# Gate sums in the prompt attention: column groups of 512 filled in two halves, one weight buffer split between groups

## The reference

```python
h = jnp.einsum('bsd,de->bse', x, w_in)     # D_MODEL 1024; the last 3*1024 columns are the gates
...
up = jnp.einsum('bsnw,nwd->bsnd', br, w_br)
mixed = (jax.nn.sigmoid(gates.reshape(B, S, 3, D_MODEL)) * up).sum(axis=2)
y = jnp.einsum('bsd,de->bse', mixed, w_o)
return _layernorm(ALPHA * x + y, ln_g, ln_b)
```

## Time and profile before

| | us |
|---|---|
| median of three runs (lowest, highest) | 3657.45 (3652.4, 3669.2) |
| the profiled execution's own time | 3665.47 |
| its span in the profile | 3663.8 |
| mean granted TensorE clock in it | 0.957 |
| TensorE matmuls busy | 3297.0, 90% of the span |
| TensorE weight loads busy | 2687.0, 73% |
| VectorE, ScalarE, GpSimd busy | 1449.7, 897.0, 172.7 |

### The profile page before, as it was taken

The page is one execution under the profiler, slowest core; times in us unless marked ns, Lnnn a source line. Parts: engine busy times, 40 slices in busy tenths (PEclk is TensorE's granted clock), DMA queues, the critical chain, the costliest instruction groups (busy, mean ns, idle before and its releaser), DMA issues. The chain is left out here.

```text
span 3663.8 us, 52922 instructions
## 1 busy us (share of the span) xinstructions
PE 3297.0 (90%) x20910; PEld 2687.0 (73%) x20910; DVE 1449.7 (40%) x3559; ACT 897.0 (24%) x2006; POOL 172.7 (5%) x118
## 2 busy tenths in 40 slices
PE   0999987999999997889969999789999999887988
PEld 0788876777777775677758888767777787755877
DVE  5214234444444442254631143444444434324446
ACT  1221212333223332120212212223332233322010
POOL 0000000101110100000000000010111110000000
PEclk9999998999999998899979999889999999988999
DMA  5322226322332317653342222352223332196433
GB/s 196 109 88 94 85 63 200 76 67 61 87 93 81 90 34 202 206 222 132 136 155 90 91 95 68 114 159 66 77 68 85 94 85 63 35 266 224 182 135 109
DMA packets 405678, 419.78 MB, mean 115 GB/s; under 512 B 155072, under 2 KB 314688, under 8 KB 403072
## 3 DMA queue, kind: packets, MB, share of 16 engines
q1 hardware_dynamic: 371600, 376.88, 33.2%
q10 hardware_dynamic: 33840, 39.66, 3.3%
HBM read 291.17 MB, written 127.64 MB: 114 GB/s over the span
## 5 line engine op out<-in xcount | busy, mean ns | idle before, releaser
L1069 PE MATMUL att_gacc<-att_gwh,keep_xh 128*128 128x256 f32 x1728 | 507.6, 294 | 6.8 <-POOL att_gwl L989 6.8
L351 PE MATMUL proj_acc<-proj_wh,keep_xh 128*128 128x512 f32 (+1 forms) x1296 | 502.1, 387 | 12.4 <-DVE proj_wl L326 12.4
L353 PE MATMUL proj_acc<-proj_wh,keep_xl 128*128 128x512 f32 (+1 forms) x1296 | 501.0, 387 | 0.0
L352 PE MATMUL proj_acc<-proj_wl,keep_xh 128*128 128x512 f32 (+1 forms) x1296 | 500.9, 387 | 0.0
L1071 PE MATMUL att_gacc<-att_gwh,keep_xl 128*128 128x256 f32 x1728 | 489.0, 283 | 0.0
L1070 PE MATMUL att_gacc<-att_gwl,keep_xh 128*128 128x256 f32 x1728 | 488.4, 283 | 0.0
L1095 ACT ACTIVATE att_p<-att_ss,att_stat 128x257 f32<-128x257 f32 (+9 forms) x384 | 249.4, 650 | 681.6 <-DVE att_stat L1145 681.6
L1023 PE MATMUL att_ss<-att_kt,att_qt 64*128 64x256 f32 (+9 forms) x1024 | 376.2, 469 | 1.4 <-DVE att_kt L1080 1.4
L1069 PEld LDWEIGHTS att_gacc<-att_gwh,keep_xh 128*128 128x128 f32 x1728 | 329.2, 191 | 22.9 <-issue 10.6
L1070 PEld LDWEIGHTS att_gacc<-att_gwl,keep_xh 128*128 128x128 f32 x1728 | 329.0, 190 | 0.0
L1071 PEld LDWEIGHTS att_gacc<-att_gwh,keep_xl 128*128 128x128 f32 x1728 | 328.1, 190 | 0.0
(11 more groups left out here) (291 smaller groups left out, 4450.3 us busy)
## 6 DMA issues: line engine op xcount, KB each, us to landing
scratch_gates<-att_gout SPq DMA_DIRECT2D x216, 128.0 KB, 1.7
up_gates<-scratch_gates SPq DMA_DIRECT2D x18, 1536.0 KB, 7.9
proj_raw<-in_w_in SPq DMA_DIRECT2D x48, 512.0 KB, 3.7
att_graw<-in_w_in SPq DMA_DIRECT2D x48, 512.0 KB
str_ka<-in_cache_a_kT SPq DMA_DIRECT2D x16, 1024.0 KB, 9.6
str_va<-in_cache_a_v SPq DMA_DIRECT2D x16, 1024.0 KB, 5.4
scratch_sg<-proj_out SPq DMA_DIRECT2D x54, 256.0 KB, 2.0
up_br<-scratch_br SPq DMA_DIRECT2D x54, 256.0 KB, 8.1
```

Source lines behind the costliest of these rows:

```text
L351: nc.tensor.matmul(bank, hi, wh[:, u, kt, 0:w], start=kt == 0, stop=False)
L352: nc.tensor.matmul(bank, hi, wl[:, u, kt, 0:w], start=False, stop=False)
L353: mm = nc.tensor.matmul(bank, lo, wh[:, u, kt, 0:w], start=False, stop=kt == KT - 1)
L1069: nc.tensor.matmul(gacc[:, 0:GW], hi, gwh[:, n % 2, k, :], start=k == 0, stop=False)
```

## The change

A group is now 512 columns (GW = 512), so there are 6 groups (GC) and each lasts two units. The places of the fills in the list stay; with 18 of them to a group, each now makes one half of a token tile's sum over channels: 12 matmuls of 512 columns over channel tiles 0 to 3 (half 0), or 4 to 7 (half 1), both into the same 512 columns of att_gacc. Only half 0 waits for g_taken, only half 1 raises g_made and is followed by the tanh and the store, both now of 512 columns. The split weights have one buffer of 512 columns instead of two of 256, the raw weights two buffers of two channel tiles by 512 columns (att_graw doubles in size, att_gwh and att_gwl keep theirs, att_gout doubles). GpSimd splits a group in four parts, and may begin the first when the last fill of the group before is done (g_made). SP loads parts 0 and 1 of the next group after the first token tile of a group and parts 2 and 3 after the last; each load waits until the part two before it is split. Half 0 of a group's first token tile waits for parts 0 and 1, half 1 for all four.

```diff
--- before.py
+++ after.py
@@ -805,6 +805,7 @@
     order = [("prep", 0, *what) for what in preparations(0)] + [("score", 0, 0), ("score", 0, 1)]
     fills = [2, 3, 4, 5, 6, 8, 10, 12, 13]
     assert len(fills) == NT
+
     for n in range(len(UNITS)):
         ahead = preparations(n + 1) if n + 1 < len(UNITS) else []
         for m in range(SUBS):
@@ -818,7 +819,8 @@
             elif m == 0 and n:
                 order.append(("back", n - 1, PT - 1))
             if m in fills:
-                order.append(("fill", n, fills.index(m)))
+                i = NT * (n % 2) + fills.index(m)
+                order.append(("fill", n // 2, i // 2, i % 2))
             if ahead and m >= 3 and m != 5:
                 order.append(("prep", n + 1, *ahead.pop(0)))
             if m % 2:
@@ -847,9 +849,9 @@
     ss, tr = ph.ps("ss", [P, 2, 1024]), ph.ps("tr", [P, 2, 512])
     oo, gacc = ph.ps("oo", [P, 512]), ph.ps("gacc", [P, 512])
     xh, xl = C["xh"], C["xl"]
-    GW = D // (H // 2)
-    graw, gout = ph.sb("graw", [P, KT // 2, GW]), ph.sb("gout", [P, 3, GW])
-    gwh, gwl = ph.sb("gwh", [P, 2, KT, GW], F32R), ph.sb("gwl", [P, 2, KT, GW], F32R)
+    GW, GC = 512, 3 * D // 512
+    graw, gout = ph.sb("graw", [P, 2, KT // 4, GW]), ph.sb("gout", [P, 3, GW])
+    gwh, gwl = ph.sb("gwh", [P, KT, GW], F32R), ph.sb("gwl", [P, KT, GW], F32R)
 
     row_loaded = ph.ring("row_loaded", RING)
     vs_loaded, sink_loaded = ph.ring("vs_loaded", 2), ph.sem("sink_loaded")
@@ -858,7 +860,7 @@
     s_made, max_ready, exp_ready = ph.sem("s_made"), ph.sem("max_ready"), ph.sem("exp_ready")
     inv_ready, pv_made, ot_ready, o_ready = (ph.sem(n) for n in ("inv_ready", "pv_made", "ot_ready", "o_ready"))
     o_stored = ph.ring("o_stored", 2)
-    gw_loaded, gw_hi, gw_lo = ph.sem("gw_loaded"), ph.sem("gw_hi"), ph.sem("gw_lo")
+    gw_loaded, gw_hi, gw_lo = ph.ring("gw_loaded", 2), ph.sem("gw_hi"), ph.sem("gw_lo")
     g_made, g_taken, g_stored = ph.sem("g_made"), ph.sem("g_taken"), ph.ring("g_stored", 3)
 
 
@@ -930,11 +932,11 @@
 
             wsrc = T["w_in"].rearrange("l (k p) n -> l p k n", p=P)
 
-            def load_gate(n, half):
-                if 2 * n + half:
-                    sp.wait_ge(gw_lo, 2 * n + half)
-                sp.dma_start(graw[:], wsrc[l, :, 4 * half:4 * half + 4, O_GATE + GW * n:O_GATE + GW * (n + 1)])\
-                    .then_inc(gw_loaded, 16)
+            def load_gate(n, part):
+                if 4 * n + part >= 2:
+                    sp.wait_ge(gw_lo, 4 * n + part - 1)
+                sp.dma_start(graw[:, part % 2], wsrc[l, :, 2 * part:2 * part + 2, O_GATE + GW * n:O_GATE + GW * (n + 1)])\
+                    .then_inc(gw_loaded[part % 2], 16)
 
             load_row(0)
             load_row(1)
@@ -943,17 +945,22 @@
             load_row(3)
             load_vs(0)
             sp.dma_start(sink[:], T["sinks"][ds(l, 1), :].to_broadcast([P, H])).then_inc(sink_loaded, 16)
-            load_gate(0, 1)
+            for part in range(1, 4):
+                load_gate(0, part)
             load_vs(1)
             for what, n, *of in order:
                 if what == "fill":
-                    t, = of
+                    t, half = of
+                    if half == 0:
+                        continue
                     sp.wait_ge(g_taken, NT * n + t + 1)
                     sp.dma_start(S["gates"][rows(t), GW * n:GW * (n + 1)], gout[:, t % 3, :]).then_inc(g_stored[t % 3], 16)
-                    if t == 0 and n + 1 < len(UNITS):
+                    if t == 0 and n + 1 < GC:
                         load_gate(n + 1, 0)
-                    if t == NT - 1 and n + 1 < len(UNITS):
                         load_gate(n + 1, 1)
+                    if t == NT - 1 and n + 1 < GC:
+                        load_gate(n + 1, 2)
+                        load_gate(n + 1, 3)
                 elif what == "prep" and of[2] == 1:
                     i = load_of[n, of[0], of[1]] + RING
                     if i < len(loads):
@@ -971,22 +978,21 @@
             for half in range(2):
                 sp.wait_ge(o_stored[half], 16 * len(UNITS))
             for part in range(3):
-                sp.wait_ge(g_stored[part], 16 * 3 * len(UNITS))
+                sp.wait_ge(g_stored[part], 16 * 3 * GC)
 
         @block.gpsimd
         def _(pool):
             for i in range(0, RING, 2):
                 nc.gpsimd.memset(row[:, i, :, HD:HD + 1], 1.0).then_inc(ones_ready, 1)
-            for n in range(len(UNITS)):
-                for half in range(2):
-                    k = slice(4 * half, 4 * half + 4)
-                    pool.wait_ge(gw_loaded, 16 * (2 * n + half + 1))
-                    if n >= 2:
-                        pool.wait_ge(g_made, NT * (n - 1))
-                    hi, lo = gwh[:, n % 2, k], gwl[:, n % 2, k]
-                    nc.gpsimd.tensor_copy(hi, graw[:]).then_inc(gw_hi, 1)
-                    pool.wait_ge(gw_hi, 2 * n + half + 1)
-                    nc.gpsimd.tensor_tensor(lo, graw[:], hi.bitcast(F32), ALU.subtract).then_inc(gw_lo, 1)
+            for n in range(GC):
+                for part in range(4):
+                    k = slice(2 * part, 2 * part + 2)
+                    pool.wait_ge(gw_loaded[part % 2], 16 * (2 * n + part // 2 + 1))
+                    if n:
+                        pool.wait_ge(g_made, NT * n)
+                    nc.gpsimd.tensor_copy(gwh[:, k], graw[:, part % 2]).then_inc(gw_hi, 1)
+                    pool.wait_ge(gw_hi, 4 * n + part + 1)
+                    nc.gpsimd.tensor_tensor(gwl[:, k], graw[:, part % 2], gwh[:, k].bitcast(F32), ALU.subtract).then_inc(gw_lo, 1)
 
         @block.tensor
         def _(pe):
@@ -1059,17 +1065,18 @@
                 bank_free(pe, g)
                 nc.tensor.transpose(tr[:, g % 2, 0:P], ot[:, a % 2, :], C["ident"][:]).then_inc(tr_made, 1)
 
-            def fill(n, t):
+            def fill(n, t, half):
                 if t == 0:
-                    pe.wait_ge(gw_lo, 2 * (n + 1))
-                if NT * n + t:
+                    pe.wait_ge(gw_lo, 4 * n + 2 * half + 2)
+                if half == 0 and NT * n + t:
                     pe.wait_ge(g_taken, NT * n + t)
-                for k in range(KT):
+                for k in range(4 * half, 4 * half + 4):
                     hi, lo = (x[:, k, rows(t)] for x in (xh, xl))
-                    nc.tensor.matmul(gacc[:, 0:GW], hi, gwh[:, n % 2, k, :], start=k == 0, stop=False)
-                    nc.tensor.matmul(gacc[:, 0:GW], hi, gwl[:, n % 2, k, :], start=False, stop=False)
-                    mm = nc.tensor.matmul(gacc[:, 0:GW], lo, gwh[:, n % 2, k, :], start=False, stop=k == KT - 1)
-                mm.then_inc(g_made, 1)
+                    nc.tensor.matmul(gacc[:, 0:GW], hi, gwh[:, k, :], start=k == 0, stop=False)
+                    nc.tensor.matmul(gacc[:, 0:GW], hi, gwl[:, k, :], start=False, stop=False)
+                    mm = nc.tensor.matmul(gacc[:, 0:GW], lo, gwh[:, k, :], start=False, stop=k == KT - 1)
+                if half:
+                    mm.then_inc(g_made, 1)
 
             for what, *of in order:
                 {"prep": prep, "score": score, "turn": turn, "value": value, "back": back, "fill": fill}[what](*of)
@@ -1101,7 +1108,9 @@
                     act.wait_ge(tr_made, g + 1)
                     nc.scalar.activation(pt[:, m % 2, 0:512], tr[:, g % 2, :], ACT.Copy).then_inc(tr_taken[g % 2], 1)
 
-            def fill(n, t):
+            def fill(n, t, half):
+                if half == 0:
+                    return
                 i = NT * n + t
                 if i >= 3:
                     act.wait_ge(g_stored[t % 3], 16 * (i // 3))
```

## The result

The changed kernel is slower, by a little: 3675.8 us median of 10 runs (3660.6 to 3686.3) against 3657.4 of the kernel before (3652.4 to 3669.2); the ratio is 1.0044, 95% interval 1.0032 to 1.0056. Timed a second time it came to 3667.1 against 3658.9, ratio 1.0023 (1.0011 to 1.0036). By the ratios it costs 8 to 16 us, where 14 us less were forecast; both medians lie above the range.

The account below looks back on a forecast made before the run. TensorE was taken to bound the prompt attention. The terms -24 - 6.5 + 13.6 + 0.5 + 1 + 1 gave -14.4 us, from a median of 3657.45 to 3643 us, with an 8-in-10 range of 3628 to 3662 us.

Parts of the forecast that it names:

- What bounds the stage: Prompt attention: TensorE, busy 727.91 of 750 us; shortening its work shortens the stage nearly one for one, waits lengthen it.
- A wide fill, 24 us: Attention fills: 12 matmuls of 512 columns instead of 24 of 256 save 0.11 us a fill, 24 us over 216.
- The prediction's own sign against it, distances well above 227 ns: Fills: starts of 512-column matmuls well above 227 ns apart would make the prediction wrong.
- Waits that go, 6.5: First fills of units 5 to 8: of 8.6 us waited for split weights, 6.5 us are gained.
- The wait that comes, 13.6: T is the end of a group's last fill; waiting for weights, second fills of units 6 and 8 add 13.6 us.
- Clock, +1: Around waits: new waits bring more half-clock stretches, removed ones take some away; -6 to +6 us, taken as +1.
- Start, 0: Start of a layer's attention: the weight parts come in time and longer weight rows can only help; 0 us.
- Tanh, +1: Fills waiting for the tanh: 0.43 us in 8 places instead of 0.22 in 16; -0.2 to +1.5, taken as +1 us.
- The rival of the single buffer: Ten boundaries between groups: late part 3 makes each wait 3.4 us more, +35 us, 3692 us; chance 0.08.

Follow-up runs that it names:

- e3: The kernel before (narrow fills) with a layer's first unit's weights kept for all units, later loads and splits left out, so it computes something else; 3647.9 us, ratio 0.9963.
- d2: The kernel before, with the second half of the next unit's weights loaded after token tile 2 instead of 8; 3648.3 us, ratio 0.9962.
- e2: The changed kernel with a layer's first group's weights kept for all groups, later loads and splits left out, so it computes something else; 3644.3 us, ratio 0.9961.
- e1: The changed kernel, but GpSimd may split parts 0 and 1, and SP loads parts 2 and 3, one fill earlier; 3645.9 us, ratio 0.996.
- d3: e1, but at a layer's start the load of part 1 waits until part 0 is split; 3642.8 us, ratio 0.9962.
- f1: d3 with att_gacc in the first PSUM bank instead of the last; 3638.3 us, ratio 0.9946.
- f3: d3 with the split weights in front of all other tiles of the stage in SBUF; 3644.2 us, ratio 0.9956.

## Why the prediction was wrong, step by step

- **What bounds the stage**: right. Every wait taken off TensorE came out in the time.
- **A wide fill, 24 us**: mis-sized by 12 us, the largest error of the sum. The distance of 512 columns was taken from the projections, 227 ns; in the attention it is 232.4, where the 256 columns had 118.6. Entering and leaving were as read. 216 x (2.953 - 2.895) = 12.5 us. The prediction's own sign against it, distances well above 227 ns, came.
- **Waits that go, 6.5**: right in place, and in the trace (6.8); the price was higher, 15 us in the stretch of units 4 to 8, as e3 and d2 show, by the clock.
- **The wait that comes, 13.6**: right in place and mechanism: T + 7.5 for part 2's split as forecast, part 3's in the first layer at T + 11.5 in unit 6 and T + 12.3 in unit 8 instead of 11.1, because its load took 4.4 and 5.2 us from issue to use instead of 3.7. The second fills wait 15.6 us in all. Nothing at units 2, 4 and 10. Its price was higher too, 25.1 and 26.5 us above e2 in the same stretch.
- **Clock, +1**: the cancelling nearly held where I looked for it. What the stretch of units 4 to 8 costs beyond its waits is 8.0 us before and 8.8 and 9.6 after. What the term left out is the layer's start: the attention of the two traces lost 8 and 13 us more than that of the kernel before, and 4.8 and 6.0 of it lie between the first transposes and unit 1's first fill.
- **Start, 0**: failed. To unit 1's first fill both layers together take 3.9 and 5.3 us more, though unit 0's fills save 1; the 1.2 GHz last 10 us longer in the first layer. I had read the stage from 641 us on, where the clock had just risen. Why it rises later is open.
- **Tanh, +1**: 2.8 us instead of 3.6, so -1.

All of it in microseconds of the traces, both layers:

| | before | changed | changed, second trace | e3 (narrow) | e2 (wide) |
|---|---|---|---|---|---|
| first transposes to unit 1's first fill | 175.8 | 179.7 | 181.0 | 174.5 | 178.6 |
| units 4 to 8 | 566.5 | 571.6 | 573.0 | 551.7 | 546.5 |
| all other units | 805.1 | 799.6 | 801.0 | 805.1 | 799.4 |

The attention grew by 3.5 and 7.8 us in the traces, where 14 less were forecast: 12 of the difference are the width, 5 to 6 the start, 2 to 3 the boundaries (10.3 and 11.7 against the 8.6 of the forecast and its clock), and 1.5 in the second trace a short fall of the clock in unit 11. The timings say 8 to 16; the rest lies in what single traces can't tell, since the trace of the kernel before was itself an execution 8 us above the median, with more of the lower clock than usual outside the attention.

The rival of the single buffer had the mechanism and the clock, but not the place: it wanted all ten boundaries, and four did it.

## What to carry to other kernels

A buffer shared between groups costs what its refill takes beyond the work that stands between the last use and the first: write that chain down as here, and shorten it at its head (release what is free earlier) before paying for a second buffer. Price a wait of a few microseconds on TensorE at more than its length where dense work follows it, for the clock falls: here 16.3 and 16.9 us of waits cost 25.1 and 26.5, half as much again, and 6.8 us of short ones cost 14.8. A price per matmul is carried from one stage to another only with a margin: 5 ns of 227 took half of this gain. Look at where a stage's window begins, for the clock may still be low there. And first look for the wait that a single moved load removes: d2, one line in the narrow kernel, has the ratio 0.9962; the wide versions without the long waits have 0.9946 to 0.9962.

## What the runs showed that was not expected

Matmuls of 512 columns with operands of the same kind and shape start 226.8 ns apart in the projections and 232.4 in the attention's fills, at 1.00 granted clock, whether GpSimd, VectorE or ScalarE work beside them or not; placing the streamed weights elsewhere in SBUF gave 230.1. The spread between runs of one kernel goes with the clock: of the ten first runs of the changed kernel the fastest, 3660.6 us, has a mean granted clock of 0.959, the slowest, 3686.3, one of 0.952. Of the versions that compute everything, e1, d3, f1 and f3 (wide) and d2 (narrow) all beat both kernels, by 0.4 to 0.5% of the kernel before.
